# Hybrid decoder layer on one core: x goes into the input projections unscaled, and its RMS factor is multiplied into their results

## The reference, cut to what matters

```
u    = rms_norm(h, mix_norm_pre)          # h * rsqrt(mean(h^2) + 1e-6) * mix_norm_pre, per token
proj = u @ w_in                            # 2048 -> 15,488 columns
c_q, c_kv, k_r, z, xbc, dt_raw, g_attn, g_ssm = split_cols(proj, IN_SPLITS)
attn = mla_branch(c_q, c_kv, k_r, ...)     # c_q and c_kv pass an rms_norm of their own first
ssm  = mamba2_branch(z, xbc, dt_raw, ...)  # conv and SiLU on xbc, softplus(dt_raw + bias), SiLU(z)
mixed = sigmoid(g_attn) * (attn @ w_attn_o) + sigmoid(g_ssm) * (ssm @ w_ssm_o)
h = h + rms_norm(mixed @ w_out, mix_norm_post)
h = h + rms_norm(SwiGLU(rms_norm(h)), ffn_norm_post)
h = h + rms_norm((p @ w_ple) * sigmoid(rms_norm(h) @ w_ple_gate), ple_norm_post)
```

## Time and profile before

| | |
|---|---|
| time, median of 3 runs | 1993.66 us |
| span of the profiled execution, first to last instruction | 1992.0 us |
| the runs' median less the span (what lies around it) | 1.7 us |
| PE busy | 1979.0 us, 99% |
| DVE busy | 1668.8 us, 84% |
| ACT busy | 1147.6 us, 58% |
| granted PE clock, mean | 0.999 |
| moved by DMA | 394.74 MB, 198 GB/s |

### The profile page before, as it was taken

How to read it: one execution, slowest core, us unless ns; L and a number is a source line. 1 busy time by engine, 2 the same in 40 slices (tenths; PEclk the granted TensorE clock), 3 DMA queues, 4 the chain that set the end, 5 groups by cost and what they waited for, 6 DMA issues and landing times.

```text
span 1992.0 us, 29428 instructions
## 1 busy us (share of the span) xinstructions
PE 1979.0 (99%) x10149; PEld 1681.0 (84%) x10149; DVE 1668.8 (84%) x2336; ACT 1147.6 (58%) x1482; POOL 18.9 (1%) x37
## 2 busy tenths in 40 slices
PE   9999999999999999999999999999999999999998
PEld 8888888888888888998888888888888888888886
DVE  7788888889888868767777787999999988888887
ACT  6666566666655545565545565556555555555575
POOL 0000000000000000000000000000000000000000
PEclk9999999999999999999999999999999999999999
DMA  8666676666566566545556667666566666766754
GB/s 235 200 191 190 190 206 184 188 192 195 172 207 209 189 203 223 156 132 156 191 191 239 205 207 242 189 202 202 190 201 200 200 201 201 254 201 207 244 189 152
DMA packets 255197, 394.74 MB, mean 198 GB/s; under 512 B 28840, under 2 KB 161440, under 8 KB 252928
## 3 DMA queue, kind: packets, MB, share of 16 engines
q1 hardware_dynamic: 251104, 369.87, 59.7%
q0 software_dynamic: 3824, 23.43, 3.5%
q10 hardware_dynamic: 176, 0.20, 0.0%
HBM read 387.08 MB, written 6.36 MB: 198 GB/s over the span
## 4 chain that ended last, share of the span: by engine, by line
PE 98%; DVE 1%; ACT 0%; DMA 0%; issue 0%; DVEq 0%; SPq 0%; ACTq 0%
PE acc L655 16%; PE acc L851 15%; PE acc L853 15%; PE acc L852 15%; PE acc L660 8%; PE acc L912 6%; PE acc L913 6%; PE acc L914 6%; PE acc L1107 1%; PE acc L785 1%; PE acc L637 1%; PE acc L636 1%; PE acc L638 1%; PE acc L1038 1%; PE acc L1242 0%; PE acc L714 0%
## 5 line engine op out<-in xcount | busy, mean ns | idle before, releaser
L1914 DVE TENSOR_TENSOR wlo<-raw,whi 128x1024 fp32r<-128x1024 f32 (+2 forms) x559 | 662.5, 1205 | 110.8 <-ACT whi L1351 108.3
L1351 ACT ACTIVATE whi<-raw 128x1024 fp32r<-128x1024 f32 (+1 forms) x560 | 572.2, 1044 | 244.4 <-PE acc L853 81.7
L655 PE MATMUL acc<-u,whi 128*128 128x512 f32 x1376 | 328.7, 391 | 0.0
L851 PE MATMUL acc<-whi,u 128*128 128x512 f32 x824 | 323.0, 392 | 0.1
L853 PE MATMUL acc<-whi,u 128*128 128x512 f32 x824 | 320.8, 389 | 0.0
L852 PE MATMUL acc<-wlo,u 128*128 128x512 f32 x824 | 320.6, 389 | 0.0
L655 PEld LDWEIGHTS acc<-u,whi 128*128 128x128 f32 x1376 | 252.7, 188 | 48.8
L851 PE MATMUL acc<-whi,g 128*128 128x512 f32 x520 | 202.8, 390 | 0.1
L853 PE MATMUL acc<-whi,g 128*128 128x512 f32 x520 | 202.4, 389 | 0.0
L852 PE MATMUL acc<-wlo,g 128*128 128x512 f32 x520 | 202.3, 389 | 0.0
L1374 ACT ACTIVATE whi<-raw 128x1024 fp32r<-128x1024 f32 x72 | 76.5, 1062 | 209.9 <-PE acc L914 162.0
(11 more groups left out here) (597 smaller groups left out, 2990.8 us busy)
## 6 DMA issues: line engine op xcount, KB each, us to landing
raw<-w_in_in SPq DMA_DIRECT2D x208, 512.0 KB, 3.8
raw<-w_gate_in SPq DMA_DIRECT2D x176, 256.0 KB, 3.0
raw<-w_up_in SPq DMA_DIRECT2D x176, 256.0 KB, 3.3
raw<-w_down_in SPq DMA_DIRECT2D x88, 512.0 KB, 4.6
raw<-w_ssm_o_in SPq DMA_DIRECT2D x64, 512.0 KB, 4.3
raw<-w_in_in SPq DMA_DIRECT2D x64, 256.0 KB, 4.0
raw<-w_attn_o_in SPq DMA_DIRECT2D x32, 512.0 KB, 4.7
raw<-w_out_in SPq DMA_DIRECT2D x32, 512.0 KB, 4.9
```

The lines of the kernel that those rows point to most:

```text
L655: return T.matmul(bank(banks[i]), wh[:, j, i * P:i * P + P], src[:, kts[j], :, :].rearrange("p a s -> p (a s)"), start=start and j == 0, s ...
L851: T.matmul(o, x_hi, wh[:, j, :], start=start, stop=False, skip_group_check=True)
L1351: S.activation(whi[:, slot, 0:w], raw[:, slot, 0:w], ACT.Copy).then_inc(sem("hi_ready"), 1)
L1914: V.tensor_tensor(wlo[:, slot, 0:w], raw[:, slot, 0:w], whi[:, slot, 0:w].bitcast(F32), ALU.subtract) \
```

## The change

- x is transposed as it landed. The scaling of x (`x_normed`) and the early sum and 1/sqrt are gone. PE's transposes wait for the loads; q = 0 and 1 are done first, q = 2 behind bc's chunk 0, q = 3 inside chunk 1. 17 warm-up products are left of 26.
- The first loads alternate: column half 0 of x for both token blocks, bc's chunks 0 and 1, column half 1 of x, chunks 2 and 3.
- ACT squares x in four pieces of 1024 columns behind the high halves of ssm chunks 0 to 3 of group 0. DVE sums them behind the tables (chunk 3), ACT does Ln and Exp at chunk 4, DVE Newton and two products with the identity (`r_diag`) at chunk 4. PE multiplies `ones` by `r_diag` behind its chunk 5, so that each partition holds all 256 factors; DVE copies them out (`r_rows`) at its chunk 5.
- DVE multiplies `r_rows` into the results: each pair of convolution inputs (128x512, three in a group), z (128x1024, one in a group), the c_q and c_kv pairs (128x512, four in all). What ACT did with `raw_sum` and `z_sum` it does with `scaled` and `z_scaled`. kr (k_rope and dt) is evacuated by DVE with the factor instead of by ACT. The two gates take the factor as the scale of their sigmoids, four calls of 512 columns instead of two of 1024.

```diff
@@ SP
-        for b in range(2):
-            for i in range(2):
+        for i in range(2):
+            for b in range(2):
                 cols = slice(1024 * i, 1024 * i + 1024)
                 sp.dma_start(x_tok[:, b, cols], x_view[b][:, cols]).then_inc(sem(f"x_in{b}{i}"), 16)
-        for slot in range(RING):
-            for src, o in zip(source("bc", 0, slot), (0, STATE)):
+            for slot in range(2 * i, 2 * i + 2):
+                for src, o in zip(source("bc", 0, slot), (0, STATE)):
...
@@ PE
         def x_transposed(q, blk):
+            pe.wait_ge(sem(f"x_in{blk}{q // 2}"), 16)
...
-        idle(26, 7)
+        idle(17, 7)
...
+            if c_ == 0:
+                x_transposed(2, 0)
+                x_transposed(2, 1)
...
+        def x_rstd_rows():
+            pe.wait_ge(sem("r_diag"), 1)
+            pe.wait_ge(sem("pv_ev"), 2)
+            for blk in range(2):
+                last = T.matmul(bank(7)[:, SEQ + blk * P:SEQ + blk * P + P], ones, r_diag[:, blk, :],
+                                start=blk == 0, stop=blk == 1)
+            last.then_inc(sem("r_mm"), 1)
...
+                if head and c_ == 5:
+                    x_rstd_rows()
@@ ACT
+        act.wait_ge(sem("pv_ev"), 1)
+        x_high(0, lambda: split("bc", 0, 0))
+        for q in range(1, 4):
+            x_high(q)
+            split("bc", 0, q)
...
-            act.wait_ge(sem("raw_sum"), it * 3 + pair + 1)
+            act.wait_ge(sem("scaled"), it * 3 + pair + 1)
...
-                act.wait_ge(sem("z_sum"), it)
+                act.wait_ge(sem("z_scaled"), it)
...
         for c_ in range(20):
             split("ssm", 0, c_)
-            if c_ == 9:
-                group_end("ssm", 0, 6)
-                S.activation(kr, bank(6)[:, 0:SEQ], ACT.Copy).then_inc(sem("kr_ev"), 1)
+            if c_ < 4:
+                x_square(c_ // 2, c_ % 2)
+            if c_ == 4:
+                rstd(st0[:, :, 2], st0[:, :, 3], "x", 1)
...
-                last = S.activation(m[:, :, cols], psum[:, 2 * half:2 * half + 2, :], ACT.Sigmoid)
+                last = S.activation(m[:, blk, cols], bank(2 * half + blk), ACT.Sigmoid, scale=r_x[:, blk:blk + 1])
@@ DVE
+        def x_rstd():
+            dve.wait_ge(sem("x_r0"), 1)
+            newton(st0[:, :, 2], st0[:, :, 3], st0[:, :, 4], "x_r", dst=r_x[:, :])
+            dve.wait_ge(sem("x_r"), 1)
+            for b in range(2):
+                last = V.tensor_scalar(r_diag[:, b, :], ident, r_x[:, b:b + 1], None, ALU.mult)
+            last.then_inc(sem("r_diag"), 1)
+
+        def x_rstd_rows():
+            dve.wait_ge(sem("r_mm"), 1)
+            link(V.tensor_copy(r_rows[:, :], bank(7)[:, SEQ:2 * SEQ]))
...
+        def by_rows(n):
+            return r_rows[:, :].unsqueeze(1).to_broadcast([P, n, SEQ])
...
             V.tensor_tensor(t[:, :, :], psum[:, b:b + 2, 0:SEQ], t[:, :, :], ALU.add).then_inc(sem("raw_sum"), 1)
+            dve.wait_ge(sem("raw_sum"), it * 3 + pair + 1)
+            V.tensor_tensor(t[:, :, :], t[:, :, :], by_rows(2), ALU.mult).then_inc(sem("scaled"), 1)
...
                 V.tensor_tensor(z[:, :, :], psum[:, 0:4, 0:SEQ], z[:, :, :], ALU.add).then_inc(sem("z_sum"), 1)
+                dve.wait_ge(sem("z_sum"), it)
+                V.tensor_tensor(z[:, :, :], z[:, :, :], by_rows(4), ALU.mult).then_inc(sem("z_scaled"), 1)
...
             split("ssm", 0, c_)
             if c_ == 3:
                 tables()
+                x_total()
+            if c_ == 4:
+                x_rstd()
+            if c_ == 5:
+                x_rstd_rows()
+            if c_ == 9:
+                rotary_dt()
```

More of the change, by code:

```diff
@@ L165, in build @@
     CONST0 = E0 + HPG * 384 * 4 + 2048
-    END = CONST0 + 7936
+    END = CONST0 + 7968
     assert END <= 229344
@@ L199, in build @@
     st = const("st", [P, 5, 4, 2])
+    r_x = const("r_x", [P, 2])
     def at(name, shape, offset, dt=F32):
@@ L219, in build @@
     st0 = first("st0", [P, 2, 8])
+    r_diag = first("r_diag", [P, 2, P])
     prep = region(G0 + 32 * 2048, G0 + 36 * 2048)
@@ L238, in build @@
     e = at("e", [P, HPG, 384], E0)
+    r_rows = at("r_rows", [P, SEQ], E0 + HPG * 384 * 4)
     sq = at("sq", [P, 4, SEQ], G0 + 32 * 2048)
@@ L688, in _ @@
         pe.wait_ge(sem("warm_set"), 1)
-        idle(26, 7)
+        idle(17, 7)
         pe.wait_ge(sem("cst_in"), 32)
         T.transpose(bank(0)[:, 0:16], rows[0:16, 0, :], cst[0:16, 0:16]).then_inc(sem("pv_mm"), 1)
-        pe.wait_ge(sem("xn_d"), 1)
         x_transposed(0, 0)
-        pe.wait_ge(sem("xn_d"), 2)
         x_transposed(1, 0)
[L696 to L699, removed]
         x_transposed(0, 1)
-        pe.wait_ge(sem("xn_d"), 5)
         x_transposed(1, 1)
-        pe.wait_ge(sem("xn_a"), 1)
-        x_transposed(2, 1)
         pe.wait_ge(sem("pv_ev"), 1)
@@ L1409, in x_square, with x_high @@
             act.wait_ge(sem(f"x_in{b}{i}"), 16)
[L1410 to L1413, removed]
+            if b or i:
+                act.wait_ge(sem("x_ssq"), 2 * b + i)
+            cols = slice(1024 * i, 1024 * i + 1024)
+            S.activation(sq_tok[:, cols], x_tok[:, b, cols], ACT.Square, accum_out=st0[:, b, i:i + 1]) \
                 .then_inc(sem("x_ssq"), 1)
[L1416 to L1421, removed]
+        def x_high(q, between=None):
             act.wait_ge(sem("xt_mm"), q + 1)
@@ L1429, in x_high @@
                              scale=pv[:, V_MIXPRE + kt:V_MIXPRE + kt + 1]).then_inc(sem("u_hi"), 1)
[L1431 to L1439, removed]
-        act.wait_ge(sem("pv_ev"), 1)
[L1441 to L1448, removed]
+                if between and j == 1:
+                    between()
+        act.wait_ge(sem("pv_ev"), 1)
+        x_high(0, lambda: split("bc", 0, 0))
+        for q in range(1, 4):
+            x_high(q)
+            split("bc", 0, q)
         def low_half(it, pair, b):
@@ L1549, in split_c @@
         def split_c(q):
-            act.wait_ge(sem("raw_sum"), GROUPS * 3 + q + 1)
+            act.wait_ge(sem("scaled"), GROUPS * 3 + q + 1)
             for i in range(2):
@@ L1571, in so_gate @@
             group_end("so", it, 15)
-            for half in range(2):
+            for half, blk in itertools.product(range(2), range(2)):
                 cols = slice(1024 * it + 512 * half, 1024 * it + 512 * half + 512)
-                last = S.activation(m[:, :, cols], psum[:, 2 * half:2 * half + 2, :], ACT.Sigmoid)
+                last = S.activation(m[:, blk, cols], bank(2 * half + blk), ACT.Sigmoid, scale=r_x[:, blk:blk + 1])
             last.then_inc(sem("sg_so"), 1)
@@ L1663, in ao_gate @@
                 act.wait_ge(sem("mixed"), 2)
-            for half in range(2):
-                last = S.activation(sg[:, :, 512 * half:512 * half + 512], psum[:, 2 * half:2 * half + 2, :], ACT.Sigmoid)
+            for half, blk in itertools.product(range(2), range(2)):
+                last = S.activation(sg[:, blk, 512 * half:512 * half + 512], bank(2 * half + blk), ACT.Sigmoid,
+                                    scale=r_x[:, blk:blk + 1])
             last.then_inc(sem("sg_ao"), 1)
@@ L2078, in _, with x_total, rotary_dt @@
         V.memset(warm[:, :], 0.0).then_inc(sem("warm_set"), 1)
[L2079 to L2096, removed]
+        def x_total():
+            dve.wait_ge(sem("x_ssq"), 4)
+            link(V.tensor_tensor(st0[:, :, 4], st0[:, :, 0], st0[:, :, 1], ALU.add))
+            V.tensor_scalar(st0[:, :, 2], st0[:, :, 4], 1.0 / D_MODEL, EPS, ALU.mult, ALU.add).then_inc(sem("x_ms"), 1)
+        def x_rstd():
[8 more added lines that the diff above has]
+            link(V.tensor_copy(r_rows[:, :], bank(7)[:, SEQ:2 * SEQ]))
+        def rotary_dt():
+            group_end("ssm", 0, 6)
+            V.tensor_tensor(kr, bank(6)[:, 0:SEQ], r_rows[:, :], ALU.mult).then_inc(sem("kr_ev"), 1)
+        def by_rows(n):
+            return r_rows[:, :].unsqueeze(1).to_broadcast([P, n, SEQ])
         def x_low(q):
@@ L2108, in x_low @@
                                        u[:, kt, 0, :].bitcast(F32), ALU.mult, ALU.subtract).then_inc(sem("u_lo"), 1)
[L2110 to L2115, removed]
         dve.wait_ge(sem("pv_mm"), 1)
         V.tensor_copy(pv[:, 0:16], bank(0)[:, 0:16]).then_inc(sem("pv_ev"), 1)
[L2118 to L2122, removed]
-        dve.wait_ge(sem("pv_ev"), 1)
[L2124 to L2128, removed]
+        dve.wait_ge(sem("pv_ev"), 1)
+        for q in range(4):
             x_low(q)
@@ L2361, in add_c_halves @@
             V.tensor_tensor(t[:, :, :], psum[:, b:b + 2, 0:SEQ], t[:, :, :], ALU.add).then_inc(sem("raw_sum"), 1)
+            dve.wait_ge(sem("raw_sum"), GROUPS * 3 + q + 1)
+            V.tensor_tensor(t[:, :, :], t[:, :, :], by_rows(2), ALU.mult).then_inc(sem("scaled"), 1)
         def split_c(q):
```

6 lines of the change are left out of this document (2 added, 4 removed).

## The result

The changed kernel takes 1996.86 us (median of 21 runs, 1996.33 to 1998.28) beside 1993.98 for the kernel before: ratio 1.0015 [1.0009, 1.0021]. In a second comparison, on another chip, it took 1996.93 beside 1993.82, 1.0017 [1.0008, 1.0026]. The forecast was 1995.5, range 1993.1 to 1997.8, "same" at 0.90: the time lies in the range, 1.4 us above the forecast. Both intervals leave out 1, so the kernel is slower, but by less than the 0.2% up to which the prediction called it "same". The profiled span went from 1992.0 to 1995.2 us.

What follows compares the result with a forecast made beforehand. PE was taken as the bound (98% of the chain), with gains only in the first 15 us. Terms -2.1 + 0.4 + 0.43 + 1.4 + 1.0 + 0.7 + 0.05 = +1.9 us gave 1995.5 us, range 1993.1 to 1997.8.

Steps and rivals of the forecast that it cites:

- First bc product: Start of the kernel: bc's first product starts at 10.3 us instead of 14.9, 4.6 us early.
- Chunk 0 of ssm: First SSM chunk: starts at 25.5 us once its late weight load lands at 23.1; 2.1 of the 4.6 us left.
- Chunk 5: Group 0: PE waits 0.4 us (0 to 0.7) for DVE's low half 5, done at 35.8 us.
- Chunks 6, 7, 8: Group 0: PE waits 1.4, 1.0 and 0.7 us because DVE's r_rows copy, sum, scaling and convolution taps precede the low halves.
- Eight groups: SSM groups: added DVE scalings lag 1.65 of 2.43 us available before masked scores are wanted, 0.8 left; cost 0.
- Cost 0 to 0.1: End of cq, near 560 us: the last scaling takes 0.72 of 0.8 us of room before PE asks.
- The gates 0, on an idle ACT: Gates: four sigmoids of 512 instead of two of 1024 on an idle ACT cost 0.
- 1: Head: first ssm load lands by 21.7 us, chunk 0 starts at 24.1, the gain arrives whole; 1993.9 us, chance 0.13.
- rival 2: Head: as rival 1, with DVE's waits at chunks 7 and 8 halved; -0.8 us, 1992.9, chance 0.05.
- 3: Eight groups: scaled operands cost DVE over 0.8 us more up to the masking; 3 to 6 us more, about 2000; chance 0.06.
- 4: Head: PE idles between 8.6 and 10.3 us and its clock falls to half; 1995.7 us, chance 0.08.
- 5: Head: weights held bc, so its first product stays at 14.9 us while the waits remain; 1998.1 us, chance 0.04.

Runs made afterwards that it cites:

- second profile: The changed kernel itself, unchanged, run and profiled once more beside other versions on the same chip: 1996.93 us.
- experiment 8: Changed kernel with group 0's side work later, row loads on ACT's queue, two-call gates: 1993.16 us; also c_q, c_kv unscaled with eps adjusted: 1992.44 us.
- experiment 6: Changed kernel with z multiplied by x's factor twice in each of the eight groups, a second full DVE pass: 2000.78 us, 1.0035.
- experiment 4: Changed kernel with the old order of first loads, four x pieces and then four of weight bc: 1999.80 us, 1.0027.

## Why the prediction held, and where it didn't

- *First bc product*: 10.99, said 10.3. The second half of the weight chunk landed at 9.60, not 9.2, and ACT wrote two parts of u ahead of the high half. It cost nothing, since the load of ssm's first chunk came last.
- *Chunk 0 of ssm*: 25.38, said 25.5, with the load landed at 22.98 (said 23.1) as the releaser. Gain 2.25 of 2.1. The fit is partly luck: the load was issued at 18.20, not 19.02, and took 4.8 us, not 4.1, and in other profiles of the same head chunk 0 came between 25.10 and 26.13.
- *Chunk 5*: no wait in the first profile, said 0.4. DVE finished low half 5 at 35.11, not 35.8: ACT's last square was done at 30.2, and the tables at 31.8. The second profile, with its earlier chunk 0, lost 0.38 there. So the term is real, and its size depends on when chunk 0 starts.
- *Products with `ones`*: 0.46, said 0.43. *Chunks 6, 7, 8*: 1.5, 1.0, 0.7 by the offset (1.24, 0.76, 0.45 idle), said 1.4, 1.0, 0.7. Offset behind them: -2.25 + 0.46 + 1.5 + 1.0 + 0.7 = +1.4 from the steps, +1.47 measured, said +1.83.
- *Chunk 9*: 49.27, said 49.5.
- *Eight groups*: 0, as said; lead 0.78 measured, 0.8 worked out.
- **"Cost 0 to 0.1" for the last scaling of cq failed.** The step gave DVE 0.72 of 0.8 us and stopped at PE's next product, where 0.13 was lost. But PE was already 1.5 late and DVE's lag stays: DVE reaches 561 us 2.2 us late and has no gap that could absorb it until 587 (it does idle, 1.46 us ahead of the low half at 579.33 for one, but for high halves whose loads start only once DVE has freed a slot), where PE in the kernel before was free of a wait by 0.14 us only (low half done at 585.26, PE behind it at 585.45). There 0.6 comes out; experiment 8 takes it away. DVE's row in the kernel before, and in the changed kernel, 2.2 later:

```profile
584.04 1.22 DVE L1914 TENSOR_TENSOR wlo<-raw,whi 128x1024 fp32r<-128x1024 f32 x1
```

```profile
586.26 1.22 DVE L1907 TENSOR_TENSOR wlo<-raw,whi 128x1024 fp32r<-128x1024 f32 x1
```

- **"The gates 0, on an idle ACT" failed.** ACT idles 4.40 us, but ahead of the high half that stands before them; from there to the last sigmoid it has no gap, and PE wants the banks at once: 0.48 us more of sigmoid is 0.5 on the path.
- The measured sum is +1.5 + 0.13 + 0.6 + 0.5 = +2.7 of the final +2.9; the forecast had +1.9. Some 0.2 us in steps of 0.15 and less (607 us the largest) were not traced. The time stayed in the range, and just inside the forecast's own (1994.3 to 1996.9), with some luck: the two terms that failed cost 1.2 us more than said, and the 0.4 of chunk 5 that the first profile did not pay hid a part of it.
- *Rivals.* 1 and 2 are false: the load came as late as said. 3 is false here, and its mechanism is shown (experiment 6: 0.52 a group once 1.2 us are added). 4 is false here and true of experiment 4. 5 is false. The sum of rival 2 had left out the 0.43 for `ones`; with it, it gives 1993.3.

## What to carry to other kernels

Work that frees the start pays only up to the next thing in line, and what it puts behind the start is priced by what it stands in front of: the same operations cost 3.3 us ahead of low halves 6 to 8, and 0.3 us, at chunk 16, when they stood two chunks later. Follow an added delay on a side engine until a gap absorbs it, not until the first product that meets it. An idle engine isn't free where it is idle because its input comes just before its output is wanted.

## What the runs showed that I had not expected

- PE idle for 1.55 us kept the clock at 1.00; for 3.23 us it lost it, and the next eight products took 1.67 us more. The order of the first loads is worth 2.9 us in the changed kernel, more than its gain at chunk 0: with it bc's products start 2.3 us earlier and at the full clock.
- The same load took 6.4 us in one profile and 6.8 in another, and chunk 0 came 1.0 us later in one profile than in another of an equal head: a single profile can't decide half a microsecond where a load is on the path.
- A wait can cost more than the idle time that the profile shows: 1.24 us of idle cost 1.5, and 0.06, too short to be listed, cost 0.3.
- On ScalarE a per-partition scale made a sigmoid of 1024 columns 88 ns longer, and four calls of 512 took 0.30 us more than two of 1024.
